# Decoder-trunk step on eight cores: query block and third tile's tokens loaded earlier, gates of three tiles and raw queries of two projected before the shift is known

## What is computed

```python
mod = silu(c) @ w_ada + b_ada                  # (b, 6D)
sh1, sc1, g1, sh2, sc2, g2 = split(mod, 6)
h = rms_norm(x) * (1 + sc1) + sh1
q, fz, i, g, gb, gc, hv = split(h @ w_in)      # 7 blocks of 512 columns
logf = log(lb + (1 - lb) * sigmoid(fz)); k = (1 - lb) * sigmoid(-fz)
o_rec, s_rec_new = hgrn2_chunked(q, k, logf, i, s_rec)     # decay scan inside chunks of 64
o_rec = rms(o_rec) * g_onorm * silu(g)
o_conv = gb * short_conv(gc * hv, s_conv, w_conv)
x = x + g1 * (concat[o_rec, o_conv] @ w_out)
h2 = rms_norm(x) * (1 + sc2) + sh2
x = x + g2 * (square(relu(h2 @ w_up)) @ w_down)
y = rms_norm(x) * g_final
```

## Time and profile before

| | us |
|---|---|
| runs | 905.5, 921.36, 905.68 |
| median | 905.68 |
| the profiled execution | 906.19 |
| its span on the slowest core (core 3) | 904.6 |
| spans of the eight cores | 895.4 to 904.6 |
| PE busy in the span | 830.9 |
| DVE, ACT, POOL busy | 478.4, 370.5, 172.0 |

### The profile page before, as it was taken

The page is one execution under the profiler, slowest core; times in us unless marked ns, Lnnn a source line. Parts: engine busy times, 40 slices in busy tenths (PEclk is TensorE's granted clock), DMA queues, the critical chain, the costliest instruction groups (busy, mean ns, idle before and its releaser), DMA issues.

```text
span 904.6 us, 17013 instructions; the slowest of 8 cores (895.4 to 904.6 us)
## 1 busy us (share of the span) xinstructions
PE 830.9 (92%) x6005; PEld 523.1 (58%) x6005; DVE 478.4 (53%) x902; ACT 370.5 (41%) x787; POOL 172.0 (19%) x229
## 2 busy tenths in 40 slices
PE   1588999999979899978799999999999999999996
PEld 1356687677666668745354565455446545654864
DVE  1365897587787877683352545244524533442422
ACT  3257874545757667531321433044213312311321
POOL 3110143343245542310001201100110021002001
PEclk9979999999998999989899999999999999999999
DMA  8999904957985731899985302210311012002101
GB/s 153 191 196 193 210 25 109 227 163 144 246 268 141 209 114 58 165 182 162 180 177 191 139 1 71 94 47 1 106 58 47 25 47 93 1 1 72 46 1 47
DMA packets 26864, 104.10 MB, mean 115 GB/s; under 512 B 3702, under 2 KB 4214, under 8 KB 22044
## 3 DMA queue, kind: packets, MB, share of 16 engines
q0 software_dynamic: 6336, 42.04, 27.6%
q1 hardware_dynamic: 18716, 54.93, 17.8%
q10 hardware_dynamic: 1728, 6.03, 2.0%
HBM read 119.47 MB, written 22.42 MB: 157 GB/s over the span
## 4 chain that ended last, share of the span: by engine, by line
PE 74%; DMA 11%; issue 5%; DVE 5%; ACT 3%; POOL 1%; DVEq 0%; SPq 0%; ACTq 0%; POOLq 0%
PE B L483 72%; DMA xn<-x 4%; DMA xe<-xp 3%; DMA ada<-w_ada 2%; ACT W L510 2%; PE B L494 1%; DVE W L527 1%; DMA gates<-xr 1%; DMA recs<-Sl 1%; DMA cB<-constB 1%; DVE hT L523 1%; DVE W L517 1%; DMA Sl<-srec 0%; DVE W L531 0%; DVE mix L517 0%
## 5 line engine op out<-in xcount | busy, mean ns | idle before, releaser
L483 PE MATMUL B<-h2T,wup 128*128 128x384 bf16 (+1 forms) x1536 | 240.2, 319 | 8.9 <-DVE uT L517 6.1
L483 PE MATMUL B<-wdn,uT 128*128 128x512 bf16 (+1 forms) x1120 | 237.5, 373 | 0.0
L510 ACT ACTIVATE W<-B 128x384 f32<-128x384 f32 (+2 forms) x241 | 118.8, 495 | 231.7 <-PE B L483 226.5
L483 PE MATMUL B<-hT,win 128*128 128x256 bf16 (+1 forms) x1728 | 202.2, 274 | 7.2 <-DMA win<-w_in 4.7
L483 PEld LDWEIGHTS B<-h2T,wup 128*128 128x128 bf16 x1536 | 151.0, 98 | 97.9 <-issue 13.0
L483 PEld LDWEIGHTS B<-hT,win 128*128 128x128 bf16 x1728 | 162.2, 100 | 33.0 <-issue 8.6
L483 PEld LDWEIGHTS B<-wdn,uT 128*128 128x128 bf16 x1120 | 109.0, 98 | 121.9
L517 DVE TENSOR_TENSOR uT<-W,B 128x384 bf16<-128x384 f32 (+1 forms) x192 | 100.7, 531 | 133.7 <-ACT W L510 112.8
L517 POOL TENSOR_TENSOR xr<-xr,W 128x512 f32<-128x512 f32 x63 | 82.3, 1307 | 434.1 <-DVE W L517 419.1
L517 DVE TENSOR_TENSOR W<-B,Gp 128x512 f32<-128x512 f32 (+1 forms) x65 | 43.9, 678 | 103.7 <-PE B L483 99.4
L483 PE MATMUL B<-wout,mix 128*128 128x512 bf16 x272 | 64.8, 389 | 7.6 <-DVE mix L517 6.9
(11 more groups left out here) (148 smaller groups left out, 642.1 us busy)
## 6 DMA issues: line engine op xcount, KB each, us to landing
x<-xr SPq DMA_DIRECT2D x17, 512.0 KB, 3.6
xn<-x SPq DMA_DIRECT2D x17, 512.0 KB, 4.1
xr<-x SPq DMA_DIRECT2D x17, 512.0 KB, 3.2
ada<-w_ada POOLq DMA_DIRECT2D x8, 1024.0 KB, 16.2
xr<-xp SPq DMA_DIRECT2D x16, 512.0 KB, 5.3
wdn<-w_down POOLq DMA_DIRECT2D x8, 1024.0 KB, 33.9
wup<-w_up POOLq DMA_DIRECT2D x8, 1024.0 KB, 22.8
yp<-xr SPq DMA_DIRECT2D x15, 512.0 KB, 2.6
```

Of the source, the lines that this page charges most:

```text
L483: ins = e.matmul(o_, lhsT=l_, rhs=r_, start=st, stop=sp_, skip_group_check=True)
L510: return P.op("act", lambda e: e.activation(out=out, in_=in_, func=func, **kw), r, w, c, prio=prio)
```

## The change

The load of win0 and of tile 2's tokens moves ahead of ada blocks 0 and 1. Tile 2 gets a third nT buffer and is treated as tiles 0 and 1 were for step A. For tiles 0 and 1 the query projection is made from the scale-only h, and its shift part, projected through win0 into `cfq`, is added on DVE head by head in the same operation that multiplies by the decay. The raw queries stay in four PSUM banks of a class of their own (H) from the projection to that operation. The transposes at the head and the modulation blocks get classes K and E with one bank each. In `steps`, F and V of tiles 0 and 1 stand behind all of the shift; the call of norm1 for tile 2 is gone.

```diff
-    CAPS = {..., "P": (0, 2), "X": (0, 8)}
-    FIFO = "PXU"
+    CAPS = {..., "P": (0, 2), "X": (0, 8),
+            "H": (4, 4), "K": (1, 1), "E": (1, 1)}
+    FIFO = "PXUH"
...
-    nT = [one("nT%d" % i, [128, 8, 256], BF16, offset=u0 + 4096 * i) for i in range(2)]
+    nT = [one("nT%d" % i, [128, 8, 256], BF16, offset=u0 + 4096 * i) for i in range(3)]
...
-            mod_bank[0] = DR.take()
+            mod_bank[0] = (EB if out_j0 < 16 else DR).take()
...
-            M, Mn = NR.take()
+            M, Mn = KB.take()
...
-        bank, bn = DR.take()
-        for hd in range(4):
-            mm([(bank[:, hd * 2:hd * 2 + 2], win[1][:, k, hd * 128:(hd + 1) * 128], shl[:, k, :], k == 0, k == 7) for k in range(8)],
-               [win_n[1], "shl"], [bn])
-        copy("dve", cfe[:], bank[:, 0:8], [bn], ["cfe"])
+        for j, c_, cn in ((1, cfe, "cfe"), (0, cfq, "cfq")):
+            bank, bn = EB.take()
+            for hd in range(4):
+                mm([(bank[:, hd * 2:hd * 2 + 2], win[j][:, k, hd * 128:(hd + 1) * 128], shl[:, k, :], k == 0, k == 7) for k in range(8)],
+                   [win_n[j], "shl"], [bn])
+            copy("dve", c_[:], bank[:, 0:8], [bn], [cn])
+            q3 = c_[:].rearrange("p (h a) -> p h a", a=2)
+            tt("dve", q3[:, :, 0:1], q3[:, :, 0:1], q3[:, :, 1:2], ALU.add, [cn], [cn])
...
-        first = kind == "p" and ti < 2
+        first = kind == "p" and ti < 3
+        early = kind == "p" and ti < 2
...
+        if early:
+            qraw = [proj(h, hn, 0, heads, TT, HB) for heads in groups]
+            yield "q"
...
-            copy("dve" if first else "act", v_[:], bank[:, :], [bn], [vn])
+            copy("dve" if early else "act", v_[:], bank[:, :], [bn], [vn])
...
+            if early:
+                bank, bn = qraw[g]
+                for i, hd in enumerate(heads):
+                    sl = slice(i * TT, (i + 1) * TT)
+                    stt(q_[:, sl], bank[:, sl], cfq[:, 2 * hd:2 * hd + 1], Eg[g][0][:, sl], ALU.add, ALU.mult, [bn, Eg[g][1], "cfq"], [qn])
+            else:
+                bank, bn = proj(h, hn, 0, heads, TT)
+                tt("dve", q_[:], bank[:, :], Eg[g][0][:], ALU.mult, [bn, Eg[g][1]], [qn])
...
     load_first(1)
+    load_in(0)
+    hs[0] = norm_first(0)
+    load_first(2)
     load_ada(0); load_ada(1)
     load_in(2)
-    for n_ in range(2):
+    for n_ in range(1, 3):
         hs[n_] = norm_first(n_)
...
-    gs = [gen(0), gen(1)]
+    gs = [gen(0), gen(1), gen(2)]
...
     steps((0, 1), "A")
+    steps((0, 1), "q")
+    mod_first(2, False)
+    steps((2,), "A")
     mod_block(0, True, 0, 0)
     mod_block(1, False, 0, 0)
     shift_first()
-    for n_ in range(2):
+    for n_ in range(3):
         mod_first(n_, True)
     steps((0, 1), "FV")
-    hs[2] = norm1(*tiles[2], eng="pool")
-    for j in (0, 3, 5, 6, 4):
+    for j in (3, 5, 6, 4):
         load_in(j)
-    gs.append(gen(2))
     steps((0, 1), "Q")
     steps((2,), "FVQ")
     steps((0, 1, 2), "G")
```

More of the change, by code:

```diff
@@ L51 @@
     BANKS = ["B%d" % i for i in range(8)]
-    CAPS = {"G": (2, 4), "M": (1, 2), "N": (0, 1), "U": (2, 3), "O": (1, 2), "D": (0, 1), "P": (0, 2), "X": (0, 8)}
-    FIFO = "PXU"
+    CAPS = {"G": (2, 4), "M": (1, 2), "N": (0, 1), "U": (2, 3), "O": (1, 2), "D": (0, 1), "P": (0, 2), "X": (0, 8),
+            "H": (4, 4), "K": (1, 1), "E": (1, 1)}
+    FIFO = "PXUH"
     def __init__(self, nc):
@@ L632, in assemble @@
     decR = Ring("dec", 3, [128, 4, 4]); decS = Ring("decs", 1, [128, 4, 16])
-    shl = one("shl", [128, 8, 2], BF16); cfe = one("cfe", [128, 8]); ecf = one("ecf", [128, 4])
+    shl = one("shl", [128, 8, 2], BF16); cfe = one("cfe", [128, 8]); ecf = one("ecf", [128, 4]); cfq = one("cfq", [128, 8])
     lbv = one("lbv", [128, 4]); oml = one("oml", [128, 4]); lnoml = one("lnoml", [128, 4])
@@ L702, in take @@
             return PSB[plan[0][k] if plan else "B0"], n
-    GA, MR, NR, UR, OR, DR, PR, GB = (Banks(c) for c in "GMNUODPX")
+    GA, MR, NR, UR, OR, DR, PR, GB, HB, KB, EB = (Banks(c) for c in "GMNUODPXHKE")
     MB2 = 1024 * 512 * 4
@@ L907, in shift_first, with proj @@
         tt("dve", shl[:, :, 1:2], v, shl[:, :, 0:1], ALU.subtract, ["modT0", "shl"], ["shl"])
-        bank, bn = DR.take()
-        for hd in range(4):
-            mm([(bank[:, hd * 2:hd * 2 + 2], win[1][:, k, hd * 128:(hd + 1) * 128], shl[:, k, :], k == 0, k == 7) for k in range(8)],
-               [win_n[1], "shl"], [bn])
-        copy("dve", cfe[:], bank[:, 0:8], [bn], ["cfe"])
+        for j, c_, cn in ((1, cfe, "cfe"), (0, cfq, "cfq")):
[6 more added lines that the diff above has]
+            tt("dve", q3[:, :, 0:1], q3[:, :, 0:1], q3[:, :, 1:2], ALU.add, [cn], [cn])
         c3 = cfe[:].rearrange("p (h a) -> p h a", a=2)
-        tt("dve", c3[:, :, 0:1], c3[:, :, 0:1], c3[:, :, 1:2], ALU.add, ["cfe"], ["cfe"])
         act(ecf[:], c3[:, :, 0:1].rearrange("p h a -> p (h a)"), AF.Exp, ["cfe"], ["ecf"], scale=-1.0)
     state = {"T": None, "dec": None, "uc": None, "mixi": 0}
-    def proj(h, hn, blk, heads, TT):
-        bank, bn = GA.take()
+    def proj(h, hn, blk, heads, TT, banks=GA):
+        bank, bn = banks.take()
         for i, hd in enumerate(heads):
@@ L986, in mixer_tile @@
         for g, heads in enumerate(groups):
-            bank, bn = proj(h, hn, 0, heads, TT)
             q_, qn = (qd2R if third else qdR).take()
-            tt("dve", q_[:], bank[:, :], Eg[g][0][:], ALU.mult, [bn, Eg[g][1]], [qn])
+            if early:
[6 more added lines that the diff above has]
+                tt("dve", q_[:], bank[:, :], Eg[g][0][:], ALU.mult, [bn, Eg[g][1]], [qn])
             qd[g] = (q_, qn)
```

## The result

| | before | changed |
|---|---|---|
| median of all runs | 906.63 (5) | 931.45 (5) |
| ratio | 1 | 1.0078, interval 1.0061 to 1.0095 |
| profiled execution, its span | 906.19, 904.6 | 913.84, 912.3 |
| ratio in a later group (e11) | 1 | 1.0062, interval 1.0043 to 1.0080 |

The change costs 6 to 7 us: 905.68 x 1.0078 is 912.7. That is under the 2% named in the prediction, but clear, and outside its range of 896.5 to 911. With intervals of 0.2% to either side, 2% was far too coarse a measure of what can be told from no change.

What follows compares the result with a forecast made beforehand. ACT was taken to bound the stretch up to tile 2's last gate: F at 66.4 plus 35.6 gives 102.0 against 104.4, less 0.5 idle, 1.9 us gained. Forecast 903.8, range 896.5 to 911.

Steps and rivals of the forecast that it cites:

- The loads: Ahead of ada 0: win0 and tile 2's tokens add 9.5 us; ada 1 lands at 56.1, win2 at 62.0.
- The estimate of 7.2 us: Loads ahead of ada 0: at 436 GB/s the 3.1 MB cost 7.2 us in place of 9.5; forecast near 901.5.
- the shift's place in PE's queue: Shift's sum after ada 1: at 57.6, +8.2 us, with ends of +7 and +10.
- the worst case: Shift's sum with the last of tile 2's step A wholly in its way on PE: +10 us.
- F: Start of the decay chain on ACT: at 66.4 in place of 55.84, after the shift, full h and a second copy and add.
- ACT as what sets the end: From F to tile 2's last gate operation: 35.6 us of ACT work and 0.5 idle, 1.9 us gained.
- PE's balance put to zero: PE around the shift: 10.7 us of work moved ahead earns no credit; idle time filled before, new idle time behind.
- The starved rival: Behind the shift: new idle time exceeds the old and the recurrence starts late; priced at 4 us, 909.7, chance 0.25.
- The rival's test: Start of the state's chain: the starved rival decides once the first state is later than 99; before, 97.28.
- the forecast's own signs: Ada 1 near 56, F near 66, ACT full to about 100, PE idle several us in 73 to 88, last gate near 102.
- The PE-bound rival: PE to 104.36: the moved work counts in full, 7 to 10 us gained, 897, chance 0.22.

Runs made afterwards that it cites:

- e11: The changed kernel itself, run again beside later runs on the same chip: ratio 1.0062 to the kernel before.
- e1: The changed kernel with step A of tile 2 recorded and tied behind the shift's projection on PE: ratio 1.0022 to the kernel before.
- e2: The changed kernel with the loads of tile 3's tokens tied behind step A of tile 2: no ratio; shift's sum at 58.5 and 60.8 on two cores.
- e9: The whole changed kernel with raw queries copied by ACT to SBUF, two banks for class H in place of four: ratio 1.0052 to the kernel before.
- e10: As e9, with the loads of tile 3's tokens also tied behind step A of tile 2: ratio 1.0020 to the kernel before.
- e6: e3 with step A of tile 2 tied behind the shift's projection on PE: ratio 0.9997 to the kernel before.
- e8: The kernel before with win0 loaded ahead of ada 0 and 1, nothing computed from it earlier: ratio 1.0050.
- e4: Query half of the change alone: win0 early, raw queries of tiles 0 and 1 in four held banks, tile 2 as before: ratio 1.0040 to the kernel before.
- e7: e4 with the raw queries copied by ACT to SBUF, two banks for class H: ratio 0.9958 to the kernel before, from three runs.
- e12: The changed kernel with tile 2's V and query projections tied behind V of tile 1 on PE: ratio 1.0075 to the kernel before.
- e3: Gates half of the change alone: tile 2's tokens and step A early, queries and win0 as before, no banks held: ratio 0.9974 to the kernel before.
- e5: e1 with raw queries copied by ACT to SBUF, two banks for H: no ratio; one usable time 914.7 against 910.0 for the kernel before.

## Why the prediction was wrong

**The loads: right for ada 1.** 9.5 us were forecast; ada 1 landed 10.1 later in the mean (45.5 and 55.6), at 54.6 on core 5 where my sum said 56.1. What the sum left out shows in win2, 11.7 later (51.4 and 63.1): a third transfer, tile 3's tokens, which the change sets free. Their buffers are read out at 43 in place of 71, and ACT's queue issues them at once. By e1 and e2 (57.9 and 56.1), e9 and e10 (57.2 and 56.3), they can cost ada 1 itself 1 to 2 us. The estimate of 7.2 us by the Trainium skill ("DMA: Bandwidth & Descriptors", section "Anatomy of one DMA") would have been further off; the rows decided rightly.

**The first step that failed: the shift's place in PE's queue.** +8.2 was forecast, up to +10 allowed, +14.8 came. My 57.6 put the sum 1.5 us behind the landing of ada 1, the worst case 3.3. It came 9.6 behind it on core 5, 8.2 in the mean, against 2.9 in the kernel before. PE had ada 0 at 56.75, then waited for the scale-only h of tile 2, did its step A from 59.63, and only then took ada 1. I had called that case the end of the range, but counted only its matmuls, not that step A itself was late: its norm was held by the 4.1 us issue on ACT, and DVE wrote its h from 56.45 on. e1 shows the price of the place, 5 us.

**F: 66.4 forecast, 71.0 came,** 6.8 behind the shift's sum in place of the 8.8 that I had; DVE put the `ecf` operations between the pieces of tile 2. A small error in the other direction.

**The second step that failed: ACT as what sets the end, with PE's balance put to zero.** ACT's sum was nearly right: from F's start to the last gate operation it took 36.4 us (71.0 to 107.4), 34.2 busy and 2.2 idle; I had 35.6 and 0.5. But that operation ended 3.1 us later than before, and the span grew by 7.7. e1 gave F at my time and was 4 us above my 903.8, and e6 moved F 3 us forward for nothing. I had said that the idle time before the shift is filled and new idle time made behind it, and took the two as equal. Up to 150 PE lost 4.8 us more than before (50.9 against 46.1): it won 2.7 from 30 to 56, and lost 2.6 more to idle time from 56 to 66 and 4.7 more from 66 to 88. How much of the 7 us each step explains, and what in the order makes PE lose it, the runs do not separate; that a later shift alone costs 3 to 6 us is e8.

**The starved rival (909.7) was nearest,** too low by 3 us. New idle time larger than the old is what came. But I had put it at 75 to 82 and to held banks; it came at 67.0 to 72.8, as a wait for DVE, and e9 frees two banks for no gain outside the noise. Banks may count in the query half (e4 against e7, 7 us). The rival's test, the first state, says nothing: e4 has it early and is slow, e12 moved it by 11 us for nothing. Of the forecast's own signs, ACT was nearly full from F on, and PE's idle time between 73 and 88 was 1.7 to 2.7 us by core, less than the several that I had named. The PE-bound rival's 7 to 10 us came nowhere; e3 and e7 gained 2.4 and 3.8.

**The clock.** What e1 and e6 pay is the low level: 32 matmuls in 6.54 us at 0.55 and in 5.02 at 0.72, in place of 3.65 at 1.00, after PE was busy 2.0 of 5.2 us and 2.4 of 4.6. The rule of the Trainium skill that I had put beside that rival ("TensorE: Matmul & The Clock Gate", section "The HAM clock gate") is that an idle array is throttled to 1.2 GHz. The traces agree in direction; the array was partly busy there, not idle.

What stays open: why the issue on ACT took 4.1 us when POOL's, at the same time, took 0.5; whether e7's gain is the banks or the order that they allow; and why e5, which joins two edits that each helped elsewhere, did not (one run). The wait for the last piece of tile 2's full h was tried only by order, not with fewer operations.

## What to carry to other kernels

Where one engine is full from some point on, price a change ahead of it by what that engine loses up to there, idle time and low clock together, as well as by the start of a chain on another engine. When a load is moved, list also the loads that its earlier use sets free (here tile 3's tokens), and look in the in-order queue for what stands ahead of the instruction that all wait for. Before computing anything from a load that is moved forward, run the move alone: here it cost most of what the whole change cost (e8). In the query half, holding half of the PSUM banks over a wait gave nothing for the work done in it, and a copy to SBUF by an idle engine gave 7 us; in the whole change the same copy gave next to nothing. Each half of this change alone (the gates as they stand, the queries with that copy) beats the whole.

## What had not been expected of the hardware

An issue of a DMA on ACT's queue took 3.1 to 4.5 us on all eight cores at 42.7 to 44.0 us, while the DMA engines were full, and 0.33 for the next at 48 to 50; in e2, at 57.7, two took 1.0. The kernel before had 0.39 at 71.85, under equally full engines. Full engines are not all of it: in e3, where the same issues stand at 42.0 to 43.0 under DMA as full, two together took 1.0 to 2.1.
